# Experts of a grouped mixture in 32-row pieces, with rows loaded ahead into two buffers and results stored by ACT

## The reference

```python
def _grouped_moe(t, router_w, router_b, w_gate, w_up, w_down):
    ...
    y = jnp.zeros(t.shape, jnp.float32)
    for e in range(N_EXPERTS):
        he = jax.nn.silu(t @ w_gate[e]) * (t @ w_up[e])
        y = y + gates[:, e:e + 1] * (he @ w_down[e]).astype(jnp.float32)
    return y.astype(t.dtype)
```

## Time and profile before

| | |
|---|---|
| median of 3 runs | 1252.38 us (1247.89 to 1255.44) |
| the profiled execution | 1254.75 us, span 1252.9 us |
| PE busy | 1048.7 us, 84% of the span |
| DVE, ACT, Pool busy | 383.7, 360.1, 86.9 us |
| moved by DMA | 317.77 MB, 254 GB/s over the span |
| mean granted clock of PE | 0.916 of full speed |

### The profile page before, as it was taken

The page is one execution under the profiler, slowest core; times in us unless marked ns, Lnnn a source line. Parts: engine busy times, 40 slices in busy tenths (PEclk is TensorE's granted clock), DMA queues, the critical chain, the costliest instruction groups (busy, mean ns, idle before and its releaser), DMA issues.

```text
span 1252.9 us, 16814 instructions
## 1 busy us (share of the span) xinstructions
PE 1048.7 (84%) x5809; PEld 663.6 (53%) x5810; DVE 383.7 (31%) x1019; ACT 360.1 (29%) x766; POOL 86.9 (7%) x145
## 2 busy tenths in 40 slices
PE   4799989988963899999999459988938987787992
PEld 2244654433443677676755356855835555454652
DVE  1356666563144000000011064778160100000112
ACT  3322255552031122122122143267021221221221
POOL 0000000000002001001011110000010110110111
PEclk9899999998965899999999769999967988888996
DMA  9930299797033189999999980050352999999953
GB/s 318 401 151 0 89 387 329 259 362 272 0 134 134 52 308 400 344 399 346 398 348 397 414 315 1 13 207 1 135 201 88 382 378 380 381 379 388 374 171 109
DMA packets 127534, 317.77 MB, mean 254 GB/s; under 512 B 5872, under 2 KB 6144, under 8 KB 127488
## 3 DMA queue, kind: packets, MB, share of 16 engines
q1 hardware_dynamic: 113680, 276.54, 59.3%
q0 software_dynamic: 12096, 40.38, 9.0%
q10 hardware_dynamic: 1712, 0.23, 0.1%
HBM read 296.68 MB, written 19.40 MB: 252 GB/s over the span
## 4 chain that ended last, share of the span: by engine, by line
PE 65%; SPq 11%; DMA 8%; DVE 7%; ACT 4%; issue 3%; POOL 1%; ACTq 1%; POOLq 0%; DVEq 0%
PE bank L584 17%; SPq L302 11%; PE bank L435 9%; PE bank L611 9%; PE bank L535 7%; DMA ring<-in_w_up_dram 4%; PE bank L378 3%; PE bank L505 3%; PE bank L476 2%; PE bank L574 2%; PE bank L488 2%; PE bank L546 1%; PE bank L444 1%; DVE h_t L1010 1%; PE bank L423 1%
## 5 line engine op out<-in xcount | busy, mean ns | idle before, releaser
L584 PE MATMUL bank<-ring,h_t 128*64 128x256 f32 (+1 forms) x2176 | 317.0, 401 | 31.1 <-DMA ring<-in_w_up_dram 28.3
L584 PEld LDWEIGHTS bank<-ring,h_t 128*64 128x64 f32 (+1 forms) x2176 | 232.3, 157 | 104.1 <-issue 44.0
L611 PE MATMUL bank<-ring,h_t 128*64 128x512 f32 (+1 forms) x544 | 151.8, 597 | 17.2 <-DVE h_t L1193 14.6
L435 PE MATMUL bank<-h_t,ring 128*128 128x512 f32 (+1 forms) x320 | 118.4, 525 | 12.3 <-ACT h_t L719 12.3
L1184 DVE COPY h_t<-bank 128x256 f32<-128x256 f32 x52 | 22.1, 424 | 338.7 <-PE bank L584 338.7
L611 PEld LDWEIGHTS bank<-ring,h_t 128*64 128x64 f32 (+1 forms) x544 | 56.5, 149 | 91.2 <-issue 91.2
L435 PEld LDWEIGHTS bank<-h_t,ring 128*128 128x128 f32 x320 | 62.6, 196 | 60.8 <-issue 41.0
L535 PE MATMUL bank<-tokm,ring 128*128 128x512 f32 (+1 forms) x256 | 85.7, 497 | 1.0 <-DVE tokm L1032 1.0
L574 PE MATMUL bank<-cst,h_t 128*128 128x128 f32 x288 | 40.6, 286 | 38.6 <-DMA h_t<-h_rows 38.6
L991 DVE RECIPROCAL work<-work 128x512 f32<-128x512 f32 (+1 forms) x20 | 54.3, 2713 | 59.5 <-ACT work L729 59.5
L1010 DVE TENSOR_REDUCE h_t<-bank 128x1 f32<-128x512 f32 (+1 forms) x96 | 57.3, 597 | 47.8 <-PE bank L476 26.5
(11 more groups left out here) (175 smaller groups left out, 1115.6 us busy)
## 6 DMA issues: line engine op xcount, KB each, us to landing
ring<-in_w_gate_dram SPq DMA_DIRECT2D x32, 2048.0 KB, 16.3
ring<-in_w_up_dram SPq DMA_DIRECT2D x32, 2048.0 KB, 22.3
ring<-in_w_down_dram SPq DMA_DIRECT2D x32, 2048.0 KB, 21.8
ring<-in_ada_w_dram SPq DMA_DIRECT2D x24, 2048.0 KB, 10.4
ring<-in_w_in_dram SPq DMA_DIRECT2D x8, 1536.0 KB, 21.9
h_t<-h_rows POOLq DMA_DIRECT2D x18, 512.0 KB, 7.1
ring<-in_w_out_dram SPq DMA_DIRECT2D x4, 2048.0 KB, 10.5
y_rows<-work POOLq DMA_DIRECT2D x52, 128.0 KB, 5.3
```

What stands on the lines that cost most here:

```text
L435: last = mm(bank[1 + i % 2][:, 0:widths[i]], qk_weights(i, k), h_t[:, k, 0:widths[i]], start=(k == 0), stop=(k == KD - 1))
L584: last = mm(o, hc_t[:, k, 0:rows], w[s][:, k, 256 * half:256 * half + 256], start=(k == 0), stop=(k == KD - 1))
L611: last = mm(o, he_t[:, k, 0:rows], wd[:, k, 512 * n:512 * n + 512], start=(k == 0), stop=(k == KF - 1))
```

## The change

Both layers' experts go in pieces of 32 rows that begin at multiples of 32 in `h_rows` and `y_rows`, so that a piece's number is its address and `short`, `chunk_row` and the sums behind them go. In layer 0 an expert has at least two pieces, in layer 1 at least one. SP zeroes both arrays from a column block of the constants' table early in layer 0.

A piece of 32 rows of 1024 is held as 128 partitions of 256: row r and quarter q at partition 4r + q after loading, at 32q + r in `yrow`. Pool loads into two halves of `hc_got`; DVE copies a half to `hc`, PE turns it with two transposes, and DVE (no longer ACT) copies it to `hc_t`. Gate and up use four column groups of 32 (two halves each of gate and up), down four groups for the quarters of the output. `he` goes to PE with one copy and two transposes. ACT evicts 128x256 and issues four stores of 32 KB itself; it waits for its own write first, and before the next eviction for the stores' landing.

In layer 0 PE's order of a piece is: gate and up of g, rows of g+1, down of g-1, turning of `he` of g (`expert_long`). In layer 1 it is plain: gate and up, rows of the next, turning of `he`, down (`expert_short`). SP asks for gate and up of expert e+3 when PE is through with gate and up of e, and for down when PE is through with down of e; the signal matmul goes.

```diff
-CHUNK = [P, SHORT]
+CHUNK = 32
+LEAST = [2, 1]
+MAX_CHUNKS = [n * NE + 2 * t * P // CHUNK for n, t in zip(LEAST, TOK_TILES)]
+ROWS = P * -(-CHUNK * (max(MAX_CHUNKS) + 3) // P)
...
+            def refill(l, e, a):
+
+                done = end_of(sp, l, e)
+                sp.wait_ge(gu_mm[l], done)
+                load_expert(l, e + 3, a, (0, 1))
+                sp.wait_ge(down_mm[l], done)
+                load_expert(l, e + 3, a, (2,))
...
                 if u == 5:
+                    for rows_dram in (h_rows, y_rows):
+                        sp.dma_start(rows_dram[:, :].rearrange("(n p) d -> p n d", p=P),
+                                     table[:, C_Z:C_ALL].unsqueeze(1).to_broadcast([P, ROWS // P, D])
+                                     ).then_inc(rows_zeroed, 16)
                     sp.wait_ge(v_mm, 2)
                     sp.wait_ge(swapped, 64)
...
+                    pe.wait_ge(hc_moved[l], n + 1)
+                    for j in range(2):
+                        last = turn(bank[5][:, P * j:P * j + P], hc[:, P * j:P * j + P], ident)
+                    last.then_inc(hc_turned[l], 1)
+
+                def gate_up(g, a):
+
+                    w = [ring[:, 3 * a + s, :].rearrange("p (k n) -> p k n", k=KD) for s in range(2)]
+                    pe.wait_ge(hc_ready[l], g + 1)
                     for k in range(KD):
+                        for q in range(4):
+                            last = mm(bank[1][CHUNK * q:CHUNK * q + CHUNK, 0:256], hc_t[:, k, :],
+                                      w[q // 2][:, k, 256 * (q % 2):256 * (q % 2) + 256],
+                                      start=(k == 0), stop=(k == KD - 1))
                     last.then_inc(gu_mm[l], 1)
...
+                def down(g, a):
+
                     wd = ring[:, 3 * a + 2, :].rearrange("p (k n) -> p k n", k=KF)
+                    pe.wait_ge(het_ready[l], g + 1)
                     pe.wait_ge(rows_ready[l], g + 1)
                     for k in range(KF):
+                        h = he_t[:, k % 2, CHUNK * (k // 2):CHUNK * (k // 2) + CHUNK]
+                        for q in range(4):
+                            last = mm(bank[4][CHUNK * q:CHUNK * q + CHUNK, 0:256], h,
+                                      wd[:, k, 256 * q:256 * q + 256], start=(k == 0), stop=(k == KF - 1))
                     last.then_inc(down_mm[l], 1)
...
+                def expert_long(e, a, turns, prev):
...
+                    with pe.Fori(g0 + 1, g1) as g:
+                        gate_up(g, a)
+                        turn_rows(g + 1)
+                        down(g - 1, a)
+                        turn_he(g)
+
+                def expert_short(e, a, turns, prev):
...
+                    with pe.Fori(g0, g1) as g:
+                        weights_in(a, turns, (0, 1))
+                        gate_up(g, a)
+                        turn_rows(g + 1)
+                        turn_he(g)
+                        weights_in(a, turns, (2,))
+                        down(g, a)
...
+                with act.Fori(0, all_chunks(act, l)) as g:
+                    act.wait_ge(he_turned[l], g + 1)
+                    do(act_g, turned_he[:, :, 0:2 * CHUNK], ACT.Silu).then_inc(silu_done[l], 1)
                     act.wait_ge(down_mm[l], g + 1)
+                    act.wait_ge(rows_stored[l], 64 * g + 64)
+                    do(yrow, bank[4][:, 0:256], ACT.Identity).then_inc(rows_ready[l], 1)
+                    act.wait_ge(rows_ready[l], g + 2)
+                    for q in range(4):
+                        act.dma_start(y_rows[bass.ds(CHUNK * g, CHUNK), 256 * q:256 * q + 256],
+                                      yrow[CHUNK * q:CHUNK * q + CHUNK, :]).then_inc(rows_stored[l], 16)
...
+                def load_rows(n, i):
+                    pool.dma_start(hc_got[:, 256 * i:256 * i + 256],
+                                   h_rows[bass.ds(CHUNK * n, CHUNK), :].rearrange("r (q c) -> (r q) c", q=4)
+                                   ).then_inc(hc_in[l][i], 16)
+
+                load_rows(0, 0)
+                load_rows(1, 1)
+                total = all_chunks(pool, l)
+                with pool.Fori(0, (total + 1) // 2) as m:
+                    for i in range(2):
+                        pool.wait_ge(hc_moved[l], 2 * m + 1 + i)
+                        load_rows(2 * m + 2 + i, i)
...
+                link(v.scalar_tensor_tensor(out=cmp3, in0=cst[:, C_G + 1:C_G + MAXCH].unsqueeze(1).to_broadcast([P, NE, MAXCH - 1]),
+                                            scalar=rows, in1=tot.unsqueeze(2).to_broadcast([P, NE, MAXCH - 1]),
+                                            op0=ALU.mult, op1=ALU.is_lt))
+                link(v.tensor_reduce(nch, cmp3, AX.X, ALU.add))
+                link(v.tensor_scalar(nch, nch, float(LEAST[l] - 1), 1.0, ALU.max, ALU.add))
...
+                with dve.Fori(0, all_chunks(dve, l)) as g:
+                    dve.wait_ge(gu_mm[l], g + 1)
+                    v.tensor_copy(he, bank[1][:, 0:256]).then_inc(he_ready[l], 1)
+                    rows_turned(g + 1)
+                    dve.wait_ge(silu_done[l], g + 1)
+                    v.tensor_tensor(he_t, act_g, turned_he[:, :, 2 * CHUNK:P], ALU.mult).then_inc(het_ready[l], 1)
+                    rows_in(g + 2)
```

More of the change, by code:

```diff
@@ L66 @@
 C_UP = C_END
-C_ALL = C_UP + P
+C_Z = C_UP + P
+C_ALL = C_Z + D
 V_ADAB = 0
@@ L249, in expert_weights, with first_of, end_of, all_chunks @@
             return [(3 * a, w_gate, KD), (3 * a + 1, w_up, KD), (3 * a + 2, w_down, KF)]
[L251 to L274, removed]
+        def first_of(engine, l, e):
+            return engine.value_load(first[0:1, bass.ds(e, 1)], min_val=0, max_val=MAX_CHUNKS[l])
+        def end_of(engine, l, e):
+            return engine.value_load(first[0:1, bass.ds(e + 1, 1)], min_val=1, max_val=MAX_CHUNKS[l])
+        def all_chunks(engine, l):
+            return engine.value_load(first[0:1, NE:NE + 1], min_val=1, max_val=MAX_CHUNKS[l])
         block = stack.enter_context(nc.Block())
@@ L344, in _ @@
                 load_expert(l, 2, 2, (0,))
-                with sp.Fori(1, 5) as i:
+                sp.wait_ge(route_ready, l + 1)
+                with sp.Fori(0, 4) as i:
                     for a in range(3):
[L347 to L350, removed]
+                        refill(l, 3 * i + a, a)
+                refill(l, 12, 0)
             for tt in range(2):
@@ L620, in experts @@
                 pe.wait_ge(route_ready, l + 1)
                 turn_rows(0)
+                expert(0, 0, 1, None)
                 with pe.Fori(0, 5) as i:
-                    for a in range(3):
-                        expert(3 * i + a, a, i + 1)
-                expert(15, 0, 6)
+                    expert(3 * i + 1, 1, i + 1, 0)
+                    expert(3 * i + 2, 2, i + 1, 1)
+                    expert(3 * i + 3, 0, i + 2, 2)
+                if LEAST[l] > 1:
+                    down(all_chunks(pe, l) - 1, 0)
@@ L886, in _ @@
         def _(pool):
-            pool.wait_ge(rows_ready[0], 1)
-            for l, rows_dram in enumerate((h_rows, y_rows)):
-                pool.dma_start(rows_dram[ROWS:ROWS + P, :], yrow).then_inc(rows_stored[l], 16)
+            for l in range(DEPTH):
+                pool.sem_inc(rows_stored[l], 64)
             for l in range(DEPTH):
                 nt = TOK_TILES[l]
-                rows = CHUNK[l]
                 pool.wait_ge(qk_done, 10 * (l + 1))
@@ L1234, in combine @@
                 add_rows(nt - 1)
-            v.memset(yrow, 0.0).then_inc(rows_ready[0], 1)
-            dve.sem_inc(rows_ready[1], 1)
+            for l in range(DEPTH):
+                dve.sem_inc(rows_ready[l], 1)
             v.memset(eps[:, 0:1], D * EPS)
```

243 lines of the change are left out of this document (71 added, 172 removed).

## The result

The changed kernel takes 1242.24 us (median of 6, 1240.27 to 1249.11), the kernel before 1251.24 (6 runs beside them): a ratio of 0.9942, 95% interval 0.9915 to 0.9968. The forecast was 1202. The profiled execution of the changed kernel is its longest, 1249.11 us with a span of 1247.4; the span before was 1252.9.

| stretch, us | before | forecast | after |
|---|---|---|---|
| to layer 0's first gate and up | 413.3 | 410.2 | 406.3 |
| experts of layer 0 | 293.5 | 274.8 | 329.3 |
| from there to layer 1's first gate and up | 240.4 | 235.9 | 233.5 |
| experts of layer 1 | 275.2 | 246 | 249.3 |
| from there to the end of the span | 30.6 | 29.1 | 29.0 |

What follows compares the result with a forecast made beforehand. PE was taken to set layer 0, with weight loads close behind, and the loads most of layer 1. Terms -21 - 32 - 3 + 2 = -54 from 1254.75 us gave 1201; 1202 was kept, range 1182 to 1285.

Steps and rivals of the forecast that it cites:

- PE's price of a piece: PE, a 32-row piece: gate and up 3.6 us, down 1.8, four transposes 0.55; sum 5.95, ends 5.8 and 6.3.
- ACT's loop: Layer 0, from one down to the next through ACT: 6.5 us, above PE's 5.95, so 6.5 is the period.
- the table load: Layer 0, in ACT's loop: 1.28 us, one a piece as before, kept by a loop body that starts with `Silu`.
- The store term: Layer 0, single `yrow`: ACT's stores land in 4.1 us, making 6.2 before the next eviction, hidden under 6.5.
- The first rival: ACT's stores held by full queues: period 9.0 us in layer 0, 1320 us in all; chance 0.20.
- The second rival: Period 7.1 to 7.4 us from stores landing in 5.3 or slower four-group steps: 1226 to 1240 us; chance 0.18.
- the third rival: PE's clock falls to 1.2 GHz in layer 1's last ten pieces: +50 us, 1252, no change; chance 0.04.
- Layer 1: Plain order, pieces of 7.1 us, first refill asked for at about 949 us: stage ends at 1190, -32 us.
- Start, ends and zeroing: Stage starts about -3 us and stage ends -1.5 in each layer; zeroing both row arrays on SP's queue +2.

Runs made afterwards that it cites:

- late turning: PE turns the next piece's rows after down, not before, against the changed kernel: 1216.4 us; with two `yrow` buffers as well: 1200.4 us.
- late refill: SP asks for gate and up of expert e+3 only after the last down of e, against the changed kernel: 1258.9 us, ratio 1.0068.
- two-piece turn: ACT's loop takes two pieces a turn, against the changed kernel: 1232.0 us with one `yrow`, 1214.7 us with two.

## Why the prediction was wrong

**PE's price of a piece** was right: 3.66 and 1.93 us against 3.6 and 1.8, and 6.19 as the shortest piece with late turning, 0.30 of it PE's stand for DVE's copy (forecast 5.95). The four column groups stream at the modulation units' rate: 3.66 us for 16 steps is 0.229 a step. The Trainium skill ("TensorE: Matmul & The Clock Gate", Part 3) has 2.38 times for three column tiles, from which the prediction estimated a step of 0.27; the trace, with four, does not bear the estimate out.

**ACT's loop is the step that failed.** Its own terms were right: eviction, own write, issues with the gap behind them (2.07 against 1.93), table load, `silu`, product, hops and down sum to 6.6 against 6.5. What it left out are two instructions that belong to another piece: DVE's copy of the rows of g+2 behind the product, and PE's turning of them ahead of down, 0.92 us with their gaps. Moving them gave pieces of 6.65 at best, and 26 us. Times 41, the period's 1.02 make 42 of the 54.5 us. 8.8 are irregular pieces: 3.3 the two downs at the lower clock, 1.0 the long issues of one piece, the others mostly store landings. The stage's two ends take the last 4, 1.6 of them its first gate and up (5.28 us in place of 3.66; the granted clock is 0.50 from 406 to 409.5 us).

**The forecast knew the table load and took it as given.** It costs a piece 1.28 us, and leaving it out shortened the loop from 7.52 to 6.24, by no more than that. Entered from the router's sigmoid, the loop had a load at the head of every turn; with one `silu` ahead of it, none was left. The Trainium skill ("ScalarE: Activation LUTs", What ACT_TABLE_LOAD costs) gives 1283 ns for a load and some 1380 ns of drain beside it. The first agrees with L817; of the second these runs show nothing.

**The store term** was close: 4.7 us of landing in layer 0 against 4.1. At a piece of 7.52 it is hidden but for a few; below 7 it ends most waits, and a second buffer was worth some 11 to 17 us.

**The first rival** (ACT's issues held by SP's) did not come at its size: four issues take 1.75 us in most pieces, also where SP stands up to 10.5 us in its own, and 2.71 at most in layer 0. Its small form is there: two issues of layer 1 took 1.0 us beside an SP in issue, and the run with the late refill lost some 9 us to long issues, most of them beside SP's. The second rival had the right size, 7.4, for the wrong reasons. The clock fell in single downs of layer 0; in the plain order's last ten pieces, which the third rival named, it stood at 0.97.

**Layer 1** came as forecast: 249.3 us against 246, 275.2 before. 10.4 of the 25.9 are the earlier first request, which the run with the late refill shows from the other side. 13 are a shorter way from that request to expert 12's `w_up`, 167.1 us against 180.1: by the shares of the queues above, rows took 9.8% of 180 us and take 6.0% of 167, 7.6 us, and weights 5.1 less. No run took the row traffic apart, so this division is argued. The last pieces gave 2.4. Part of the agreement is luck: expert 12's `w_up` let PE go 172.8 us after the stage's start against 174.5 forecast, but the ten pieces behind it took 76.5 against some 71, since the first gate and up took 6.10 us and the changes of expert 0.8 to 1.3 each.

**Start, ends and zeroing:** from DVE's mask to the first gate and up 24.2 us after 26.8, -2.5 where -3 was forecast; the end -1.6 for -1.5. The other 4.5 us ahead of layer 0's experts lie before routing, in code that the change hardly touches; the runs here, but for the doubled zeroing, start that stage between 402 and 407 us. The zeroing, priced at +2, is hidden: its queue is empty from about 125 us on. The forecast's sum, less the 2.4 us that it names, is 1198 and not 1202, which changes no term.

## What to carry to other kernels

Where engines run in order, the length of a loop is found by walking every instruction that stands between its steps on each engine, those for the next piece too; a short one for the next piece behind the last step of this one is paid in full, though its engine is idle four fifths of the time. When a loop gets shorter, ask at once what stands right behind it (here a buffer's landing, then PE), and mind that an edit meant for one of them may change another, as the two-piece turn did to the table load. A pipelined order is worth its name only if its loop is shorter than the plain order's.

## What was not expected of the hardware

A function table was loaded anew in every turn of a loop that uses one table only, 65 times and 83.4 us in all, and one small activation ahead of the loop removed it. Most of ACT's issues kept 0.32 us beside an SP that stood 10 us in issue, but in the run with the late refill a piece's four took 2.6 to 3.2 us eleven times, nine of them with SP's requests in the same moment. Single downs of 3.2 to 3.6 us in place of 1.93, at a granted clock of 0.50, come between pieces at full clock, each behind a stand of PE of 1.8 to 2.5 us in place of 1.04; not every such stand has one behind it, and which pieces they hit differs from run to run.
